# A small bf16 product of zeros ahead of each group's up products, in both MLP loops

## What is computed

```python
# first block; D_FF = 2816
def swiglu(h, w_gu, w_down):
    a, b = jnp.split(h @ w_gu, 2, axis=-1)
    return (jax.nn.silu(a) * b) @ w_down

# second block; D_FF_2 = 4096
h2 = _rms_norm(x, g_pre_mlp[l])
m = jnp.square(jax.nn.relu(h2 @ w_up[l])) @ w_down[l]
x = x + _rms_norm(m, g_post_mlp[l])
```

## Time and profile before

| | |
|---|---|
| median of 3 executions | 822.99 us (822.92 to 823.28) |
| span of the profiled execution, first to last instruction | 821.9 us |
| TensorE busy with products | 797.3 us, 97% |
| TensorE loading weights | 695.4 us, 85% |
| VectorE, ScalarE, GpSimd busy | 428.3, 418.8, 376.9 us |
| first MLP, first loop product to last down product | 264.78 to 441.33 us |
| second MLP, the same | 640.56 to 815.32 us |

### The profile page before, as it was taken

The page is one execution under the profiler, slowest core; times in us unless marked ns, Lnnn a source line. Parts: engine busy times, 40 slices in busy tenths (PEclk is TensorE's granted clock), DMA queues, the critical chain, the costliest instruction groups (busy, mean ns, idle before and its releaser), DMA issues.

```text
span 821.9 us, 14292 instructions
## 1 busy us (share of the span) xinstructions
PE 797.3 (97%) x5493; PEld 695.4 (85%) x5493; DVE 428.3 (52%) x684; ACT 418.8 (51%) x641; POOL 376.9 (46%) x181
## 2 busy tenths in 40 slices
PE   6999999999899999999999999999999999999996
PEld 4778877887778999999998889999887988899985
DVE  4675568984667533422336747645455333423435
ACT  5335426455846444444444955654756544444443
POOL 3126000000164654666545986565464554666452
PEclk9999999999999999999999999999999999999999
DMA  9984577134953666555654796434455556566551
GB/s 320 302 285 133 161 235 253 54 102 103 345 168 116 198 193 190 175 179 185 192 166 132 227 205 186 130 105 132 150 167 167 157 182 197 180 190 191 184 149 51
DMA packets 94397, 146.61 MB, mean 178 GB/s; under 512 B 15742, under 2 KB 64111, under 8 KB 94353
## 3 DMA queue, kind: packets, MB, share of 16 engines
q1 hardware_dynamic: 92896, 143.23, 55.9%
q0 software_dynamic: 1424, 2.77, 1.3%
q10 hardware_dynamic: 32, 0.01, 0.0%
HBM read 144.93 MB, written 1.06 MB: 178 GB/s over the span
## 4 chain that ended last, share of the span: by engine, by line
PE 85%; DVE 6%; issue 3%; POOL 2%; ACT 2%; DMA 2%; DVEq 0%; SPq 0%; ACTq 0%; POOLq 0%
PE bank L1877 82%; POOL w_lo L628 2%; ACT w_hi L693 1%; PE bank L2147 1%; PE bank L1968 1%; DMA raw<-in_w_mod 1%; DMA x<-in_x 1%; DMA gate_mlp_b<-gate_rows 1%; DVE x L1829 1%; PE bank L2455 1%; DVE w_lo L1196 1%; DVE stat L1513 1%; DVE x L1642 0%; DVE o_lo L1734 0%; DVE bank L1641 0%
## 5 line engine op out<-in xcount | busy, mean ns | idle before, releaser
L628 POOL TENSOR_TENSOR w_lo<-raw,w_hi 128x1024 fp32r<-128x1024 f32 (+2 forms) x150 | 361.8, 2428 | 318.7 <-ACT w_hi L693 318.5
L693 ACT ACTIVATE w_hi<-raw 128x1024 fp32r<-128x1024 f32 (+1 forms) x218 | 226.1, 1045 | 217.3 <-PE bank L1877 192.5
L1196 DVE TENSOR_TENSOR w_lo<-raw,w_hi 128x1024 fp32r<-128x1024 f32 x71 | 87.0, 1236 | 141.3 <-ACT w_hi L693 141.2
L1877 PE MATMUL bank<-z_hi,w_hi 128*128 128x256 f32 x384 | 109.0, 284 | 0.2
L1877 PE MATMUL bank<-z_hi,w_lo 128*128 128x256 f32 x384 | 107.2, 279 | 0.0
L1877 PE MATMUL bank<-z_lo,w_hi 128*128 128x256 f32 x384 | 107.1, 279 | 0.0
L1877 PE MATMUL bank<-n_hi,w_hi 128*128 128x256 f32 x352 | 100.4, 285 | 1.0 <-POOL w_lo L628 1.0
L1877 PE MATMUL bank<-n_hi,w_lo 128*128 128x256 f32 x352 | 99.8, 284 | 0.0
L1877 PE MATMUL bank<-n_lo,w_hi 128*128 128x256 f32 x352 | 99.0, 281 | 0.0
L1877 PE MATMUL bank<-w_hi,mlp_h_hi 128*128 128x512 f32 x216 | 85.3, 395 | 0.0
L1877 PE MATMUL bank<-w_hi,mlp_h_lo 128*128 128x512 f32 x216 | 85.2, 395 | 0.0
(11 more groups left out here) (419 smaller groups left out, 1553.0 us busy)
## 6 DMA issues: line engine op xcount, KB each, us to landing
raw<-in_w_in SPq DMA_DIRECT2D x54, 512.0 KB, 4.5
raw<-in_w_down SPq DMA_DIRECT2D x54, 512.0 KB, 3.7
raw<-in_w_gu SPq DMA_DIRECT2D x44, 512.0 KB, 3.5
raw<-in_w_up SPq DMA_DIRECT2D x32, 512.0 KB, 3.7
raw<-in_w_mod SPq DMA_DIRECT2D x24, 512.0 KB, 4.1
raw<-in_w_mod SPq DMA_DIRECT2D x32, 256.0 KB, 6.1
raw<-in_w_out SPq DMA_DIRECT2D x12, 512.0 KB, 4.0
raw<-in_w_in SPq DMA_DIRECT2D x8, 336.0 KB, 3.0
```

The source lines that it names most:

```text
L628: nc.gpsimd.tensor_tensor(wl[:, w % SPL, 0:size], raw[:, slot_raw, 0:size], wh[:, w % SPL, 0:size].bitcast(F32), ALU.subtract).then_inc(s_ ...
L693: nc.scalar.activation(wh[:, w % SPL, 0:size], raw[:, slot_raw, 0:size], ACT.Copy).then_inc(s_hi, 1)
L1196: V.tensor_tensor(wl[:, w % SPL, :], raw[:, slot_raw, :], wh[:, w % SPL, :].bitcast(F32), ALU.subtract).then_inc(s_lod, 1)
L1877: return nc.tensor.matmul(out_, l, r_, start=start, stop=stop, skip_group_check=True)
```

## The change

A helper is added, and a call of it in each loop, behind the group's wait and ahead of its up products. The stationary matrix is `zb`, 128 x 128 zeros in bf16; the moving columns are the first n of the bf16 identity; the result, zeros, is added to the first n columns of bank 4. n is 8 and 32 for the two groups of a trip of the first loop, and 8, 32 and 64 for the three of the second. Nothing else changes, on no engine.

```diff
+            def nothing_added(bank, n):
+
+                mm(ps[bank][:, 0:n], zb[:], idb[:, 0:n], False, False)
+
...
                     else:
                         pe.wait_ge(s_h, 2 + 2 * i)
+                    nothing_added(4, (8, 32)[v])
                     up(4 + 6 * v, i, 2 * (1 - v))
                     down(8 + 6 * v, i, v, v)
...
                     pe.wait_ge(s_relu, 1 + v + 3 * i)
+                    nothing_added(4, (8, 32, 64)[v])
                     up2(2 + 4 * v, 1 + v, i)
                     down2(4 + 4 * v, v, i)
```

## The result

The kernel with the 25 products takes 826.27 us, the median of 11 executions (825.25 to 827.96), against 823.71 us for the kernel before in the same number (822.29 to 826.79). The ratio is 1.0036, with a 95% interval of 1.0024 to 1.0048: slower by 3.0 us (2.0 to 4.0); the two medians alone are 2.6 us apart. I had forecast 1.2 us and called it the same. The kernel of before is itself 0.7 us slower by these 11 executions than by the 3 that I had (822.99 us).

The account below looks back on a forecast made before the run. The prediction took TensorE alone to bound both MLP loops. 2.5 us of product cost less 1.3 us of pace gain made 1.2 us, taking the median from 822.99 to 824.2 us, range 819.9 to 826.3.

Parts of the forecast that it names:

- What bounds the kernel: In both MLP loops only TensorE counts; what it gains or loses there reaches the end one for one.
- The price of a product: Each added product costs TensorE 0.11 us whatever its width; 23 of the 25 counted, 2.5 us of cost.
- open load: At each added product, the next up matrix's load has no long product to run beside, standing open about 0.11 us.
- the two products behind the zero blocks: Added products right behind blocks of zero products, where a load is open already: counted as costing nothing, at worst 0.11 each.
- The pace behind it: Nine first-MLP up groups go at 0.1185 us a product instead of 0.1200 behind an open load: 1.3 us of gain.
- The sum: Over both MLPs, 2.5 us of cost less 1.3 us of gain makes 1.2 us slower, counted as the same.
- the pace stays: Rival: nine first-MLP groups keep 0.1200, so 2.5 us of cost stand alone, 825.5 us; chance 0.2.
- The three signs: TensorE's timeline: second up product 0.09 to 0.14 us later; up groups of 11.5 us in first MLP, 5.77 in second.
- One sign of failure: The prediction fails if, among other signs, up groups of the second MLP change their pace at all.
- The fast pace: Rival: up groups move to 0.1135 us a product; 819.9 us for the first MLP, 817.0 with the second; chance 0.2.
- The dearer product: Rival: steps between bf16 and float32 cost at both seams, 0.20 us a product, 826.3 us; chance 0.1.
- the nearly free one: Rival: the load is hidden and only columns count, 0.3 us in all; 822.0 us, or 823.3 without the pace; chance 0.1.

Follow-up runs that it names:

- e8: One float32 product of 8 columns per place instead of the bf16 one, against the kernel of before: 17.086 us a group in the first MLP; second MLP alternates 11.37 and 11.15.
- e0: The kernel of before profiled again, unchanged: span 821.1 us, 16.97 us a group in the first MLP.
- e2: The bf16 products added in the second MLP's loop only, against the kernel of before: ratio 1.0017, 1.4 us slower.
- e6: The same bf16 products put between a group's up and down products, against the kernel of before: 17.10 and 11.375 us a group.
- e7: The kernel of before profiled a third time, unchanged: span 820.2 us.
- e10: The kernel of before profiled a fourth time, unchanged: span 821.8 us.
- e13: One float32 product of 128 columns per place, against the kernel of before: 17.087 us a group in the first MLP, 11.367 in the second.
- e11: The float32 product of 8 columns per place run a second time, same code: up groups of the second MLP alternate as they did the first time.

## Why the prediction was wrong, point by point

- **What bounds the kernel: right.** TensorE alone counts in both loops; no other engine shows in its waits within the loops but at the first product of the first, and each loop's loss reaches the end (1.0015 and 1.0017 make 1.0036 within their intervals).
- **The price of a product, 0.11 us: right in kind, too small in size.** It is 0.133. The first float32 product costs 0.114 to 0.120 by e8, so 0.11, read from the row of three small products, was at most 0.01 too low for the open load. The other 0.014 to 0.019 comes with the bf16 matrix. I wrote that the zeros "load beside the last down product"; they don't, as the PEld rows of the change show. That this is what the 0.014 to 0.019 pays for was not shown. That the width doesn't matter held up to 256 columns. 23 x 0.023 = 0.5 us of the miss. That the two products behind the zero blocks cost nothing was right.
- **"The pace behind it", 1.3 us of gain: the step that failed.** The text took the first MLP's 0.1200 for the kernel's normal state and the 0.1185 of the loop's first group for the effect of an open load at its start. The profile of the change has the 0.1187 that was forecast, and so have e0, e2, e6, e7 and e10, with no product ahead of the up groups. And e13's first group starts with the open load and goes at 0.1200. On the kernel's usual pace there was nothing to gain: 1.3 us of the miss. Two things stay open: what picks the pace, and whether the added products would have sped up an execution like the one in the first profile, since none of the profiles with a product ahead of the up groups has 0.1200 in a later group, and without one it was one profile in six (with e6).
- **The sum.** 2.5 - 1.3 = 1.2 us became 3.07 - 0 = 3.07. The rival "the pace stays" (2.5 us, 825.5) had the right form of the sum for another reason: the pace doesn't change, not because it stays slow, but because it was fast all along. I gave it 0.2, half the chance of the forecast.
- **What would show it.** The three signs that I had named were all met in the profile of the change: the open load, first-MLP groups of 11.48 us (11.5 named), second-MLP groups of 5.74 (5.77 named). One sign of failure was met too, that a group of the second MLP changes its pace, in the first group of its loop; it was worth nothing, as shown above. The signs compared one profile with another, and so couldn't tell a gain from an odd base. What would have warned me stood in the text itself: several paces for one kind of product, and no row that says what picks one.
- **The other rivals.** The fast pace of 0.1135 does occur in the loops, in every other group of e8, but not behind bf16 products, except in the first group of the second loop of the change. The dearer product (0.20) and the nearly free one are both out by the 0.133 measured, with 8 columns and with 256. The dearer one's 826.3 us equals the measured median by luck: a price too high, a gain that didn't come, and a base 0.7 us too low. By the same luck the median still lies within my range, whose upper end is that rival.

## What to carry to other kernels

In this kernel a product slipped between two others costs TensorE the load of the *next* stationary matrix, about 0.12 us here between float32 matrices, and almost nothing for its columns, up to the 256 tried. Look at the load rows to see which load has a product to run beside, and which has none. And where one kind of product goes at several fixed paces within a trace, the base itself may be one of several: take a second profile of the unchanged kernel before counting a change of pace as a gain.

## What the runs showed of the hardware that I had not expected

- 256-column float32 products with a new matrix each go at one of four paces, 0.1133, 0.1177, 0.1187 or 0.1200 us, all with the granted clock at 1.00. Each has its own repeating steps, in ns: 113, 113, 114 in the fast groups of e8; 115, 118, 122, 120, 119 at 0.1187 in e0; 118, 120, 122 at 0.1200 in the first profile. The same code took 0.1200 in one profile and 0.1187 in three. What picks the pace was not settled.
- The load of a bf16 matrix did not run beside the float32 product ahead of it (PEld idle 0.28 us, then the load with its own product), while the load of a float32 matrix did (e8).
- A second bf16 product of 8 to 64 columns costs 0.02 to 0.027 us, a second float32 one of 8 columns 0.10 to 0.11.
- The same wait of 1.6 us was followed by a granted clock of 0.50 in e8 (219.5 to 222.5 us) and of 1.00 in e11, with the same code.
